# Gated DeltaNet heads: the samples' output product moves from the last inverse level to the end of the chunk pass

## The reference, cut to what matters

```python
def step(S, inp):                      # one chunk; a sample's four tokens are one chunk
    uc, wc, qc, ac, kc, glc = inp
    v_new = uc - wc @ S                # needs the inverse of the chunk's lower triangle
    o = qc @ S + ac @ v_new            # the output product
    S = glc * S + kc.T @ v_new         # decay, then update
    return S, o
```

## Time and profile before

| | us |
|---|---|
| median of 3 runs (lowest, highest) | 1932.34 (1927.18, 1936.38) |
| the profiled execution | 1930.3 |
| its span | 1928.5 |
| PE busy in the span | 1816.5 |
| DVE busy in the span | 1119.8 |
| ACT busy in the span | 546.5 |

### The profile page before, as it was taken

How to read it: one execution, slowest core, us unless ns; L and a number is a source line. 1 busy time by engine, 2 the same in 40 slices (tenths; PEclk the granted TensorE clock), 3 DMA queues, 4 the chain that set the end, 5 groups by cost and what they waited for, 6 DMA issues and landing times.

```text
span 1928.5 us, 34430 instructions
## 1 busy us (share of the span) xinstructions
PE 1816.5 (94%) x13511; PEld 1740.1 (90%) x13511; DVE 1119.8 (58%) x1814; ACT 546.5 (28%) x1008; POOL 490.8 (25%) x279
## 2 busy tenths in 40 slices
PE   7999999999999999999999999999989899999997
PEld 7988888898999999998888888888888799999997
DVE  6777777764616161677666666666653562626275
ACT  5544444423000000125334334334421300000011
POOL 3000000002656565550000000000000365656562
PEclk9999999899999999999899899899889899999999
DMA  6222222222232322232121121021112232322321
GB/s 200 69 66 70 66 63 66 64 75 69 81 89 87 88 87 87 87 79 56 35 69 39 36 63 44 26 67 46 34 47 66 63 91 81 90 84 87 87 88 58
DMA packets 258002, 137.41 MB, mean 71 GB/s; under 512 B 6762, under 2 KB 256068, under 8 KB 257924
## 3 DMA queue, kind: packets, MB, share of 16 engines
q1 hardware_dynamic: 220544, 117.23, 21.0%
q10 hardware_dynamic: 37380, 19.06, 3.5%
HBM read 124.27 MB, written 12.00 MB: 71 GB/s over the span
## 4 chain that ended last, share of the span: by engine, by line
PE 80%; DVE 11%; ACT 4%; issue 4%; ACTq 1%; DVEq 0%; DMA 0%
PE pj L511 59%; PE rr L613 2%; PE rr L807 2%; PE rr L532 2%; PE rr L549 2%; PE rr L800 2%; PE rr L771 1%; DVE ol L2024 1%; DVE w_lo L1556 1%; DVE pr L1782 1%; PE rr L706 1%; PE rr L789 1%; PE rr L652 1%; PE rr L659 1%; PE rr L716 1%
## 5 line engine op out<-in xcount | busy, mean ns | idle before, releaser
L472 POOL TENSOR_SCALAR w_hi<-w_raw 128x1024 fp32r<-128x1024 f32 x134 | 141.8, 1058 | 1403.6 <-PE pj L511 1375.8
L511 PE MATMUL pj<-xh,w_hi 128*128 128x272 f32 x2064 | 466.1, 308 | 10.3 <-DVE w_lo L1556 4.6
L511 PE MATMUL pj<-xh,w_lo 128*128 128x272 f32 x2064 | 438.1, 295 | 0.0
L511 PE MATMUL pj<-xl,w_hi 128*128 128x272 f32 x2064 | 437.6, 294 | 0.0
L511 PEld LDWEIGHTS pj<-xh,w_hi 128*128 128x128 f32 x2064 | 334.1, 195 | 32.4 <-issue 19.6
L474 POOL TENSOR_TENSOR w_lo<-w_raw,w_hi 128x1024 fp32r<-128x1024 f32 x134 | 345.5, 2578 | 11.2
L511 PEld LDWEIGHTS pj<-xl,w_hi 128*128 128x128 f32 x2064 | 335.5, 195 | 0.0
L511 PEld LDWEIGHTS pj<-xh,w_lo 128*128 128x128 f32 x2064 | 334.5, 195 | 0.0
L511 PE MATMUL pj<-oh,w_hi 128*128 128x272 f32 x1248 | 265.1, 294 | 5.8 <-DVE w_lo L1556 3.1
L511 PE MATMUL pj<-oh,w_lo 128*128 128x272 f32 x1248 | 259.6, 290 | 0.0
L511 PE MATMUL pj<-ol,w_hi 128*128 128x272 f32 x1248 | 259.2, 289 | 0.0
(11 more groups left out here) (325 smaller groups left out, 2315.0 us busy)
## 6 DMA issues: line engine op xcount, KB each, us to landing
w_raw<-in_mlp_w_up_dram SPq DMA_DIRECT2D x64, 512.0 KB, 4.0
w_raw<-in_mlp_w_down_dram SPq DMA_DIRECT2D x64, 512.0 KB, 3.5
w_raw<-in_hgrn_w_in_dram SPq DMA_DIRECT2D x32, 512.0 KB, 4.0
w_raw<-in_gdn_w_in_dram SPq DMA_DIRECT2D x32, 512.0 KB, 4.1
out_dram<-S ACTq DMA_DIRECT2D x16, 512.0 KB, 3.4
w_raw<-in_hgrn_w_out_dram SPq DMA_DIRECT2D x9, 512.0 KB, 3.7
w_raw<-in_gdn_w_out_dram SPq DMA_DIRECT2D x9, 512.0 KB, 3.6
S<-in_state_hgrn_dram ACTq DMA_DIRECT2D x8, 512.0 KB, 4.1
```

Of the source, the lines that this page charges most:

```text
L472: nc.gpsimd.tensor_scalar(w_hi[:, s], w_raw[:, j], 1.0, 1.0, ALU.mult, ALU.mult).then_inc(hi_pool, 1)
L511: last = mm(pj[:, s, b, 0:HALF], w[:, s, k, :], v[:, k, b * HALF:(b + 1) * HALF], start=(k == 0 and a == 0), stop=(k == end - 1 and a == 2))
```

## The change

PE issues `os` after the last `dS3` and before its wait for `S3`, into another PSUM bank (bank 0, columns 256 to 287, in place of bank 1). The waits for `vns` and `tt32` that stood before it are gone, and `w` no longer waits for ACT's `os`; `dSs0`, which writes bank 0, does. ACT copies `os` out after its last copy of the chunk pass, just before `oo`. DVE's `sdec` moves from behind `S0` to behind `inverse`, ahead of the `low` that stood there. Nothing is computed in another way, and no instruction is added or removed but waits.

```diff
@@ lists of DVE, ACT and PE
-                "vbig", "S0", "sdec", "S1", "S2", "S3", "sn0", "sn1"],
+                "vbig", "S0", "S1", "S2", "S3", "sdec", "sn0", "sn1"],
...
-            gr=["x2", "x4", "x8", "x16", "x32", "rs", "vns", "x64", "os",
-                "vn0", "w", "vn1", "vn2", "vn3", "oo", "sq"],
+            gr=["x2", "x4", "x8", "x16", "x32", "rs", "vns", "x64",
+                "vn0", "w", "vn1", "vn2", "vn3", "os", "oo", "sq"],
...
@@ PE, gdn_rec
-                    if m == 64:
-                        pe.wait_ge(s.sem, s.after("vns", h))
-                        pe.wait_ge(v.sem, v.after("tt32", h))
-                        mm(rr[:, 1, 0:TS], oo[0:TS, VNS:VNS + P], A[0:TS, TP:T], start=True, stop=False)
-                        for b in range(NSEQ):
-                            last = mm(rr[:, 1, b * SLEN:(b + 1) * SLEN], S0[:, b, :],
-                                      qe[:, TP + b * SLEN:TP + (b + 1) * SLEN], start=False, stop=(b == NSEQ - 1))
-                        t.did(last, "os")
                     more(2)
...
                         t.did(mm(rr[:, 0, 0:P], Tt[:, cols], vT[:, cols], start=True, stop=True), "vn0")
-                        pe.wait_ge(s.sem, s.after("os", h))
...
+                mm(rr[:, 0, 256:256 + TS], oo[0:TS, VNS:VNS + P], A[0:TS, TP:T], start=True, stop=False)
+                for b in range(NSEQ):
+                    last = mm(rr[:, 0, 256 + b * SLEN:256 + (b + 1) * SLEN], S0[:, b, :],
+                              qe[:, TP + b * SLEN:TP + (b + 1) * SLEN], start=False, stop=(b == NSEQ - 1))
+                t.did(last, "os")
                 pe.wait_ge(v.sem, v.after("S3", h))
...
                 later(1)
+                pe.wait_ge(s.sem, s.after("os", h))
                 t.did(mm(rr[:, 0, :], kdTs[:], gd_vbig[0], start=True, stop=True), "dSs0")
@@ ACT, gdn_head
-                    if m == 64:
-                        sem_of(t, "os", h)
-                        s.did(f(oo[:, TP:T], rr[:, 1, 0:TS], ACT.Copy), "os")
...
+                sem_of(t, "os", h)
+                s.did(f(oo[:, TP:T], rr[:, 0, 256:256 + TS], ACT.Copy), "os")
                 sem_of(t, "o", h)
@@ DVE, gdn_head
-                    if c == 0:
-                        after(t, "os", h)
-                        v.did(decay_samples(eGs[:, NC:]), "sdec")
...
                 if nxt is not None:
                     gdn_prepare("inverse", nxt)
-                    if not final:
-                        low(nxt, U_GIN + 6)
+                after(t, "os", h)
+                v.did(decay_samples(eGs[:, NC:]), "sdec")
+                if nxt is not None and not final:
+                    low(nxt, U_GIN + 6)
```

More of the change, by code:

```diff
@@ L287, in build @@
             gr=["x2", "dt2", "dtt2", "vT", "x4", "dt4", "dtt4", "kT", "x8", "sks", "dt8", "dtt8", "x16", "dt16", "dtt16",
-                "srt", "x32", "dt32", "dtt32", "svn", "x64", "os", "dt64",
-                "vn0", "w", "dS0", "vn1", "dS1", "vn2", "dS2", "vn3", "dS3", "o", "dSs0", "dSs1"],
+                "srt", "x32", "dt32", "dtt32", "svn", "x64", "dt64",
+                "vn0", "w", "dS0", "vn1", "dS1", "vn2", "dS2", "vn3", "dS3", "os", "o", "dSs0", "dSs1"],
             gf=["ss"],
```

## The result

The changed kernel takes 1960.75 us (median of 5 runs, 1957.99 to 1963.08) against 1932.21 us before (5 runs): ratio 1.0155, 95% interval 1.0133 to 1.0177, or 28.5 us slower. The prediction of 1946 had the sign right, and its range, up to 1958, missed the time by 3 us. The profiled execution took 1959.4 us (span 1957.6), 29.1 more than the one before.

The account below looks back on a forecast made before the run. PE was taken as the bound. Place A +3.9 - 0.05 - 2.14 and Place B +11.5, with +1.6 for new half clock, gave +14.8 us, 1945.1 profiled or 1947.1 by median; predicted 1946, range 1934 to 1958.

Parts of the forecast that it names:

- Place A: From `x64` to `S0`: +3.9 us in heads 0 to 5, -0.05 in head 6, -2.14 in head 7.
- c: Time from the end of `pred64` to DVE's `S0`: 5.66 us mean in heads 0 to 3, forecast 6.08 after.
- lower bound of 3.9 us: Half clock after PE's restart behind `pred64`: at least 3.9 us, read behind 2.00 us of idling; 4.6 was taken.
- Place B: End of the chunk pass: the moved product makes `o` 1.42 us later in head 1, +11.5 us in all heads.
- The decay and the waits added: DVE's moved decay, 1.21 us per head, is covered by idling before `sn1`; the added waits cost nothing: each 0.
- The sign named for it: If right, DVE's idling before `sn1`, 2.76 us, would be shorter with the decay moved; no size given.
- the term for new half clock from `o` on: Behind the moved product, one head gets a 3.4 us stretch at half clock: +1.6 us, ends 0 and 12.8.
- The reading behind that term: Level 8's eight similar products were read as all at full clock; 1 of 9 products was followed by half clock.
- The third: Rival: the clock falls behind the moved product at the chunk pass's end in most heads, +26 us, 1956; chance 0.10.
- The second: Rival: each head keeps its half clock behind `pred64`, only the overhang goes, +4.4 us, 1934.7; chance 0.13.

Follow-up runs that it names:

- Experiment 4: Changed kernel with eight unread full-clock matmul calls filling PE's gap ahead of the wait for `pred64` in heads 0 to 6: 1.0069 of the kernel before.
- experiment 2: Kernel before with the samples' output product made a second time, unread, at the end of the chunk pass: 1.0073 of the kernel before.
- experiment 3: Kernel before with only the decay of the sample states moved behind the next head's `inverse`: 0.9998 of the kernel before.
- experiment 18: Changed kernel with the product's sixteen 4-column state matmuls replaced by unread full-clock matmuls of 1150 columns: 1.0167 of the kernel before.
- experiment 1: Changed kernel without the sixteen 4-column state matmuls of the moved product, samples' output incomplete: 1.0068 of the kernel before.
- experiment 5: Kernel before with the samples' product moved behind the next head's `kk`, ahead of the wait for `pred64`: 1.0065 of the kernel before.
- experiment 10: Changed kernel with DVE's `sr1` moved ahead of the convolution, removing PE's wait in level 8: 1943.25 us, 1.0082 of the kernel before.
- experiment 12: Kernel before with the samples' product and first filler tile ahead of the wait for `pred64`, and `sr1` ahead of the convolution: 1910.74 us, 0.9906.
- experiment 11: Changed kernel with `sr1` ahead of the convolution and eight unread matmul calls filling the gap ahead of `pred64`: 1938.11 us, 1.0049 of the kernel before.
- experiment 17: Changed kernel with unread full-clock matmuls of 950 columns ahead of the samples' product at the end of the chunk pass: 1.0157 of the kernel before.

## Why the prediction was wrong, point by point

- **Place A**, forecast +3.9 - 0.05 - 2.14 = +1.7 us: by the two stages it is -2.2 + 3.9 = +1.7. The sum is right, in part by luck. The gap was 4.2 us (4 forecast), half clock between `pred64` and `S0` 3.4 us (in head 3 5.9) and not 4.6, so heads 0 to 5 lost 2.1 us and not 3.9; head 6 then came at half clock, and its c rose from 2.76 to 4.48. Its lower bound of 3.9 us was misread: behind level 8's 2.00 us half clock lasts 3.4 us. Experiment 4 shows the mechanism.
- **Place B**, forecast +11.5: 12.2 us by the stage, +14 alone (experiment 2). Right, but for a slip without weight: head 6's product before takes 2.14 us like head 7's, not 2.11.
- **The decay and the waits added**, 0: right (experiment 3). The sign named for it, a shorter idling before `sn1`, did not come: 2.76 us before and after.
- **The chunk passes**, which had no term, took 2.5 us more, in heads 6 and 7, at a lower clock.
- **The step that failed** is the term for new half clock from `o` on. I took one stretch of 3.4 us behind the moved product in one head, +1.6 us, and gave the levels, whose work is unchanged, no term and no reason for none. In its place the stage from `o` to the next `svn` cost +11.0 us, by 31.6 us more half clock at 0.36 us each: 20.5 us of it begin right behind the moved product, in heads 3 and 6 (17.1 in head 6 alone), and 13.7 us more than before begin behind level 8's product (2.5 us left over from a chunk pass before are gone). With 11.0 for 1.6, and the chunk passes, the sum is 1.7 + 11.5 + 11.0 + 2.5 = 26.7 of the 27.4 that the heads lost.
- **The reading behind that term** was wrong. I wrote that level 8's products are all at full clock in and just behind them, and that 1 of 9 such products was followed by half clock. In the kernel before, the clock falls 0.8 us behind the first of the eight (at 934.89, for 6.8 us) and 0.95 us behind the seventh, here with PE busy without a break, for 10.2 us (the product in the timeline, then busy time by stretch):

```profile
1362.12 1.90 PE L781 MATMUL rr<-ws,S 128*128 128x4 f32 x16
...
1362.00:1364.90 2.90, 2.90 (x27) 2.90 (x27) 2.87 (x7) 1.08 (x5) 0.00 (x0) 1.00 0.00 0
1365.00:1375.20 10.20, 9.47 (x41) 8.82 (x40) 8.16 (x17) 2.19 (x4) 0.00 (x0) 0.50 0.00 0
```

By the measure that counted head 6's `os`, it was 3 of 9, for up to 10.2 us. The wait in that level 8 is 0.73 us and lies inside this stretch, so the 2.00 us were followed by half clock five times, not six.

- **The rivals.** The third, a fall of the clock at B in most heads, named a time close to the measured one (1956) and was right in kind for heads 3 and 6; in the other heads with a successor the clock right behind the product is full, and experiment 18 is as slow without the light product, so the nearness of its time is luck. The second, the clock as it was, is refuted by the rows. **The Trainium skill**, by "TensorE: Matmul & The Clock Gate" (Part 1, on the clock gate), would have left the clock out as a penalty under 1% of a span; here half clock is 178 of 1930 us before, and the clock term alone is 11 us of 28.5. The same section of the Trainium skill says that the watch on activity runs freely, so that the same kernel measures a different count of slow matmuls from run to run; the mean clocks of the 109 runs of the kernel before, 0.945 to 0.963, agree.

What is shown: beside B's delay some 13 us come with place A (experiments 1 and 5), without need of the light product at B (18). In the profiles of the change and of experiment 5 the levels lose by half clock, with PE's work unchanged, and in the change's profile all of the increase begins behind the two 4-column products. Experiments 1 and 18 show the half clock in their runs, but their profiles do not put it all there. What is not shown: why place A brings it in most forms (1 and 5 alone; 10 with B) and not in experiment 12, while delays at B of the kernel before do not. Neither the gap (4), nor level 8's idling (10), nor both (11) is its sole cause. That level 8's product is the seat of A's part is an open rival, which a run with that product moved or padded would test.

## What to carry to other kernels

Where PE's clock falls and returns within a loop, unchanged work is not unchanged cost: a shift of 1 to 4 us per iteration came with 11 us more in a stage whose PE work the edit did not touch. Look for runs of very short matmuls there, not for idling alone. So price an edit there with a clock term of about that size in both signs, and read the mean clock of every run, not of one profile. A small step queued behind a long one, for which PE idles, is the safer gain: moving 0.18 us of DVE work took 12 us off.

## What the runs showed of the hardware that was not expected

- The same 2.00 us of idling, ahead of the same instructions, was followed by half clock after 0.1 us for 6.8 us, or after 1.8 us for 3.4 us.
- PE's clock fell while PE was busy without a break: 0.95 us behind sixteen 4-column matmuls (the level 8 that follows head 5 in the kernel before), to half for 10.2 us.
- Work may be free for the clock's sake: 12.8 us more of it in experiment 17 changed nothing in the time, with 33 us less half clock.
- A kernel's run-to-run spread here goes with the clock: 1913 to 1940 us for the kernel before, with a mean granted clock of 0.945 to 0.963. Over 272 executions, each kernel taken by itself, the time rises by 0.36 us for each us of half clock.
